# Two-tile blocks: where the split of the next block's second chunk, the copy out of PSUM and the row sums stand

## What is computed

```python
h = rmsnorm(x, pre_norm_mix)
z = h @ w_in                     # gated units, q, k, v, og, gates, m_a, m_b
y_a = spatial_gating(u, layernorm(vs), ...)
y_b = rmsnorm(gla_chunked(q, k, v, log_a)) * silu(og)
merged = sigmoid(m_a) * (y_a @ w_proj_a) + sigmoid(m_b) * (y_b @ w_proj_b)
x = x + rmsnorm(merged @ w_out, post_norm_mix)
q = rmsnorm(x, pre_norm_xa) @ wq;  k = rmsnorm(mem) @ wk;  v = rmsnorm(mem) @ wv
x = x + rmsnorm(softmax(q @ k.T) @ v @ wo, post_norm_xa)
hid = conv3(rmsnorm(x, pre_norm_ffn) @ w_up) + conv_b
gate, up = split(hid)
x = x + rmsnorm((gelu(gate) * up) @ w_down, post_norm_ffn)
```

## Time and profile before

| | us |
|---|---|
| median of 3 runs | 3876.51 (3867.89 to 3877.65) |
| the profiled execution, whole | 3870.68 |
| its span, first to last instruction | 3868.9 |
| TensorE busy within the span | 3625.0 |

### The profile page before, as it was taken

How to read it: one execution, slowest core, us unless ns; L and a number is a source line. 1 busy time by engine, 2 the same in 40 slices (tenths; PEclk the granted TensorE clock), 3 DMA queues, 4 the chain that set the end, 5 groups by cost and what they waited for, 6 DMA issues and landing times.

```text
span 3868.9 us, 46318 instructions
## 1 busy us (share of the span) xinstructions
PE 3625.0 (94%) x18672; PEld 2939.7 (76%) x18672; DVE 2013.4 (52%) x3121; ACT 1672.2 (43%) x2723; POOL 67.9 (2%) x118
## 2 busy tenths in 40 slices
PE   7899999999898999999999999999999799999998
PEld 2667777887776777777777777766777599999776
DVE  1666654344466746642355544445555466666444
ACT  2323344444422424455544334445445555555433
POOL 1200000000020000000000000000000000000000
PEclk8999999999999999999999999999999999999999
DMA  9643321233364455323355555534555256555554
GB/s 361 187 151 109 104 60 50 61 101 105 99 194 158 148 183 166 88 64 109 92 183 161 160 176 177 180 109 161 184 174 179 93 171 187 187 186 186 180 185 163
DMA packets 351045, 577.49 MB, mean 149 GB/s; under 512 B 25316, under 2 KB 131060, under 8 KB 348912
## 3 DMA queue, kind: packets, MB, share of 16 engines
q1 hardware_dynamic: 344512, 549.47, 44.8%
q0 software_dynamic: 6320, 25.06, 2.3%
HBM read 570.26 MB, written 4.19 MB: 148 GB/s over the span
## 4 chain that ended last, share of the span: by engine, by line
PE 56%; DVE 4%; ACT 3%; DMA 2%; issue 1%; DVEq 0%; SPq 0%; ACTq 0%
PE ps L706 36%; PE ps L1601 13%; PE ps L1283 1%; DVE w_lo L675 1%; DMA raw_ring<-in_w_in_dram 1%; ACT w_hi L669 1%; PE ps L1195 1%; PE ps L1081 1%; PE ps L1168 1%; PE ps L1177 0%; PE ps L743 0%; PE ps L1474 0%; PE ps L1479 0%; DMA raw_ring<-in_w_proj_b_dram 0%; PE ps L1191 0%
## 5 line engine op out<-in xcount | busy, mean ns | idle before, releaser
L675 DVE TENSOR_TENSOR w_lo<-raw_ring,w_hi 128x1024 fp32r<-128x1024 f32 (+1 forms) x827 | 1007.4, 1223 | 1173.5 <-ACT w_hi L669 1172.2
L669 ACT CAST w_hi<-raw_ring 128x1024 fp32r<-128x1024 f32 (+1 forms) x827 | 861.4, 1048 | 1218.2 <-PE ps L706 496.1
L706 PE MATMUL ps<-w_hi,r_a 128*128 128x512 f32 x3552 | 1311.6, 408 | 56.6 <-DVE w_lo L675 20.3
L706 PE MATMUL ps<-w_lo,r_a 128*128 128x512 f32 (+1 forms) x2624 | 1041.6, 397 | 0.0
L706 PE MATMUL ps<-w_hi,r_b 128*128 128x512 f32 (+1 forms) x2272 | 864.6, 399 | 17.6 <-DVE w_lo L675 10.8
L706 PEld LDWEIGHTS ps<-w_hi,r_a 128*128 128x128 f32 x3552 | 677.6, 191 | 242.6 <-issue 56.5
L706 PEld LDWEIGHTS ps<-w_lo,r_a 128*128 128x128 f32 x2624 | 502.4, 191 | 113.4 <-issue 8.1
L706 PEld LDWEIGHTS ps<-w_hi,r_b 128*128 128x128 f32 x2272 | 436.7, 192 | 126.6 <-DVE w_lo L675 16.5
L1601 PE MATMUL ps<-r_a,w_hi 128*128 128x256 f32 x2816 | 498.6, 279 | 0.0
L1601 PEld LDWEIGHTS ps<-r_a,w_hi 128*128 128x128 f32 x2816 | 430.8, 188 | 0.0
L1601 PE MATMUL ps<-r_a,w_lo 128*128 128x256 f32 x1408 | 394.5, 280 | 0.0
(11 more groups left out here) (335 smaller groups left out, 2949.9 us busy)
## 6 DMA issues: line engine op xcount, KB each, us to landing
raw_ring<-in_w_in_dram SPq DMA_DIRECT2D x386, 512.0 KB, 3.6
raw_ring<-in_ffn_w_up_dram SPq DMA_DIRECT2D x176, 512.0 KB, 3.5
raw_ring<-in_w_ada_dram SPq DMA_DIRECT2D x128, 512.0 KB, 3.8
raw_ring<-in_w_out_dram SPq DMA_DIRECT2D x96, 512.0 KB, 3.5
raw_ring<-in_ffn_w_down_dram SPq DMA_DIRECT2D x88, 512.0 KB, 3.5
gla_arena<-in_w_ada_dram SPq DMA_DIRECT2D x64, 512.0 KB, 9.2
raw_ring<-in_w_proj_b_dram SPq DMA_DIRECT2D x32, 512.0 KB, 3.5
raw_ring<-in_w_proj_a_dram SPq DMA_DIRECT2D x16, 512.0 KB, 3.5
```

Of the source, the lines that this page charges most:

```text
L669: nc.scalar.copy(WH[:, ph.s_slot(i, j), 0:n], RAW[:, ph.raw_slot(i, j), 0:n]).then_inc(hi_ready, 1)
L675: nc.vector.tensor_tensor(WL[:, ph.raw_slot(i, j), 0:n], RAW[:, ph.raw_slot(i, j), 0:n], WH[:, ph.s_slot(i, j), 0:n].bitcast(F32), ALU.sub ...
L706: mm = nc.tensor.matmul(PS[:, t, a:z], X(x, k, t), W[w][:, kk * cols + a:kk * cols + z], start=(k == 0 and q == 0), stop=(c == len(js) - 1 ...
```

## The change

It leaves every instruction of TensorE and its order; it changes where some instructions of ScalarE and VectorE stand, and two waits of TensorE. In the two-tile products the copy out of a block is put behind the split of the next block's second chunk. In "xk" the two sums of squares are put behind the third and the fourth split, and what hangs on them moves one chunk on, so that the last of four wide VectorE operations falls into "xv". In "down" the sums of squares go behind the fourth split. The pieces of the last "up" block are dealt between the first splits of "down"; TensorE waits for the block before the last alone, and for the last just ahead of chunk 21, which reads it.

```diff
@@ -1608,13 +1608,17 @@
             for i in range(11):
                 up_body(i)
 
-            pe.wait_ge(up_free, 88)
-            pe.wait_ge(up_lo, 44)
+            pe.wait_ge(up_free, 84)
+            pe.wait_ge(up_lo, 42)
 
             def dn_body(i):
                 for b in range(2):
-                    pe_block(pe, PH["down"], i, list(range(22 * b, 22 * b + 22)), 2, NB,
-                             lambda x, k, t: AT[:, x, k, t * P:t * P + P], range(2), acc_at("down", i, 2, b))
+                    js = list(range(22 * b, 22 * b + 22))
+                    for c in range(22):
+                        if (i, b, c) == (0, 0, 21):
+                            pe.wait_ge(up_lo, 44)
+                        pe_block_part(pe, PH["down"], i, js, c, 2, NB,
+                                      lambda x, k, t: AT[:, x, k, t * P:t * P + P], range(2), acc_at("down", i, 2, b))
             for i in range(2):
@@ -1680,7 +1684,7 @@
                 def body(i):
                     for q, j in enumerate(js):
                         act_hi(act, ph, i, j)
-                        if q == 0 and evac and i:
+                        if q == 1 and evac and i:
                             evac(i - 1)
                 for i in range(first, ph.iters):
@@ -2047,17 +2051,16 @@
                 ph = PH[name]
 
                 def body(i):
-                    if not (skip and i == 0):
-                        for j in range(9):
-                            act_hi(act, ph, i, j)
-                        sig_evac(name, i)
-                    for j in range(9, js):
+                    for j in range(9 if skip and i == 0 else 0, js):
                         act_hi(act, ph, i, j)
+                        if j == 9 and not (skip and i == 0):
+                            sig_evac(name, i)
                 for i in range(4):
                     body(i)
             act_hi(act, PH["ma"], 0, 0)
+            act_hi(act, PH["ma"], 0, 1)
             uv_evac(3)
-            for j in range(1, 4):
+            for j in range(2, 4):
@@ -2092,7 +2095,7 @@
             def q_body(i, evac, steps=()):
                 for j in range(8):
                     act_hi(act, ph, i, j)
-                    if j == 0 and evac:
+                    if j == 1 and evac:
@@ -2178,7 +2181,7 @@
             for i in range(4):
                 for j in range(0 if i else 9, 16):
                     act_hi(act, ph, i, j)
-                    if j == 8:
+                    if i and j == 9:
@@ -2192,7 +2195,7 @@
             for i in range(4):
                 for c in range(8):
                     act_hi(act, PH["wo2"], i, c)
-                    if i and c == 0:
+                    if i and c == 1:
@@ -2204,18 +2207,26 @@
             def x_evac(name, dst):
                 evac_to(name, PH[name], 7, 2, lambda t, b: dst[:, t, :])(0)
 
+            def y_squares(t):
+                ins = nc.scalar.activation(JUNK2, Y2[:, t], ACT.Square, accum_out=SS[:, t:t + 1])
+                if t == 0:
+                    L(ins)
+                else:
+                    ins.then_inc(ss_ready, 1)
+
             for j in range(8):
                 act_hi(act, PH["xk"], 0, j)
-                if j == 0:
+                if j == 1:
                     wo2_evac(3)
                     act.wait_ge(acc_free, AC["xk"][0][0])
                     act.wait_ge(rt_ready, NI["p_mix"])
-                    squares([(JUNK2, Y2[:, t], SS[:, t:t + 1]) for t in range(2)], ss_ready)
-                if j == 3:
+                if j in (2, 3):
+                    y_squares(j - 2)
+                if j == 4:
                     root("p_mix", SS[:, 0:2], RINV[:, 0:2])
             for j in range(8):
                 act_hi(act, PH["xv"], 0, j)
-                if j == 0:
+                if j == 1:
@@ -2241,24 +2252,28 @@
             warm_root()
             ph = PH["xo"]
 
-            def evac_squares(name, y, i, b, j):
+            def evac_y(name, y, i, b, j):
+                st, n = acc_at(name, i, 2, b), 2 * i + b
+                for t in range(2):
+                    gemm_wait(act, st, t, 2, PH[name], i, j)
+                    nc.scalar.copy(y[:, t, n * NB:n * NB + NB], PS[:, t, :]).then_inc(acc_free, 1)
+
+            def evac_squares(name, y, i, b):
                 st, n = acc_at(name, i, 2, b), 2 * i + b
                 cols = slice(n * NB, n * NB + NB)
-                for t in range(2):
-                    gemm_wait(act, st, t, 2, PH[name], i, j)
-                    nc.scalar.copy(y[:, t, cols], PS[:, t, :]).then_inc(acc_free, 1)
                 act.wait_ge(acc_free, st[0] + 2)
                 part_squares(y[:, 0, cols], 0, n, JUNKB)
                 part_squares(y[:, 1, cols], 1, n, JUNKB, y_sq if n < 3 else ss_ready)
 
             def xo_evac(i, b):
-                evac_squares("xo", Y2, i, b, 2 * b + 1)
+                evac_y("xo", Y2, i, b, 2 * b + 1)
+                evac_squares("xo", Y2, i, b)
             for i in range(2):
                 for b in range(2):
                     act_hi(act, ph, i, 2 * b)
+                    act_hi(act, ph, i, 2 * b + 1)
                     if i or b:
                         xo_evac(*((i, 0) if b else (i - 1, 1)))
-                    act_hi(act, ph, i, 2 * b + 1)
             act_hi(act, PH["up"], 0, 0)
             act_hi(act, PH["up"], 0, 1)
@@ -2315,22 +2330,26 @@
                             fn(pi, pb, q)
             for i in range(11):
                 up_body(i)
-            for c in range(8):
-                for fn, q in pieces.get(c, []):
-                    fn(10, 1, q)
-
-            ph = PH["down"]
+
+            pd = PH["down"]
 
             def dn_evac(i, b):
-                evac_squares("down", YF, i, b, 22 * b + 21)
+                evac_y("down", YF, i, b, 22 * b + 21)
             for i in range(2):
                 for b in range(2):
+                    before = (i, 0) if b else (i - 1, 1)
                     for q in range(22):
-                        act_hi(act, ph, i, 22 * b + q)
-                        if q == 0 and (i or b):
-                            dn_evac(*((i, 0) if b else (i - 1, 1)))
+                        act_hi(act, pd, i, 22 * b + q)
+                        if (i, b) == (0, 0):
+                            for fn, k in pieces.get(q, []):
+                                fn(10, 1, k)
+                        elif q == 1:
+                            dn_evac(*before)
+                        elif q == 3:
+                            evac_squares("down", YF, *before)
             warm_root()
             dn_evac(1, 1)
+            evac_squares("down", YF, 1, 1)
@@ -2390,7 +2409,7 @@
                     for q, j in enumerate(js):
                         if not (i == 0 and q < done):
                             dve_lo(dve, ph, i, j)
-                        for fn, at in ((evac, 1 if own else 0), (later, 3)):
+                        for fn, at in ((evac, 1), (later, 3)):
                             if fn and q == at and i:
@@ -3002,7 +3021,7 @@
             for i in range(4):
                 for j in range(0 if i else 9, 16):
                     dve_lo(dve, PH["mb"], i, j)
-                    if i and j == 0:
+                    if i and j == 1:
@@ -3038,21 +3057,20 @@
 
             for j in range(8):
                 dve_lo(dve, PH["xk"], 0, j)
-                if j == 2:
+                if j == 3:
                     mean_eps("p_mix", 2, D)
-                if j == 4:
+                if j == 5:
                     mean_rinv("p_mix", 2)
                     dve.wait_ge(pn_in, 16)
-                if j in (4, 6):
-                    t = (j - 4) // 2
-                    L(V.scalar_tensor_tensor(Y2[:, t], Y2[:, t], RINV[:, t:t + 1], PN, ALU.mult, ALU.mult))
                 if j in (5, 7):
                     t = (j - 5) // 2
-                    ins = TT(X2[:, t], X2[:, t], Y2[:, t], ALU.add)
-                    if t == 1:
-                        ins.then_inc(mixed, 1)
+                    L(V.scalar_tensor_tensor(Y2[:, t], Y2[:, t], RINV[:, t:t + 1], PN, ALU.mult, ALU.mult))
+                if j == 6:
+                    TT(X2[:, 0], X2[:, 0], Y2[:, 0], ALU.add)
             for j in range(8):
                 dve_lo(dve, PH["xv"], 0, j)
+                if j == 0:
```

More of the change, by code:

```diff
@@ L3040, in _ @@
                 dve_lo(dve, PH["xk"], 0, j)
-                if j == 2:
+                if j == 3:
                     mean_eps("p_mix", 2, D)
-                if j == 4:
+                if j == 5:
                     mean_rinv("p_mix", 2)
                     dve.wait_ge(pn_in, 16)
-                if j in (4, 6):
-                    t = (j - 4) // 2
-                    L(V.scalar_tensor_tensor(Y2[:, t], Y2[:, t], RINV[:, t:t + 1], PN, ALU.mult, ALU.mult))
                 if j in (5, 7):
                     t = (j - 5) // 2
-                    ins = TT(X2[:, t], X2[:, t], Y2[:, t], ALU.add)
-                    if t == 1:
-                        ins.then_inc(mixed, 1)
```

(5 more changed lines are left out.)

## The result

| | before | changed |
|---|---|---|
| median, us | 3877.08 (4 runs, 3867.89 to 3881.06) | 3846.39 (4 runs, 3840.55 to 3852.16) |
| ratio, 95% interval | | 0.9926 (0.9911 to 0.994) |
| span of the profiled execution | 3868.9 | 3849.4 |

The changed kernel is faster by 0.74%, some 29 us. The forecast was 3849.5. The spans differ by only 19.5 us, and the first question is why that is less.

What follows compares the result with a forecast made beforehand. TensorE, busy 3625.0 of 3868.9 us, bounds the kernel, so only its waits at edited places count. Eight terms sum to 27.0 us, taken from a median of 3876.5 to give 3849.5 us; range 3836 to 3862.

Steps and rivals of the forecast that it cites:

- Part 1: Plain block boundaries in "uv", "ma", "qkvo", "mb", "wo2": a stall of 0.35 us vanishes at 12.75 boundaries, +4.5 us.
- Part 2: Table loads going with the copy, first "uv" and third "mb" block: stall 0.65 instead of 0.35, twice, -0.6 us.
- Part 3: VectorE's copies in "ma" and "mb" come late: 2.0 and 2.6 us lost, -4.6; bounds nothing to a loss of 5.3.
- Part 4: "wo2": the turned tile goes ahead of the block's copy, removing TensorE's wait for transposed halves, +1.7 us.
- Part 5: "xk" and start of "xv": a 7.7 us loss shrinks to small losses of 0.7, +7.0 us; bounds 5 to 7.7.
- Parts 6 and 8: Block boundaries: "xo" three at 1.9 us, +5.7 (half, 2.9, if splits are late); "down" three at 1.84, +5.5.
- Part 7: From "up" to "down": 5.55 us wait for the first w_lo and 2.2 of half clock go, +7.8; lower end 6.5.
- (A): Rival: VectorE's six late copies bring the clock down, 2.8 us each; gain only 10, 3866 us; chance 0.05.
- (B): Rival: queues further behind than counted (table loads, late w_lo in "xv" or "xo"); gain 17 to 24; inside the forecast's 0.85.
- (C): Rival: the stall only moves, TensorE waits in the third chunk instead of the second; within 0.3%, 3870 us; chance 0.04.
- (D): Rival: late HBM transfers hold the second split and the copy behind it; 2.1 us to spare; slower, 3909; chance 0.03.

Runs made afterwards that it cites:

- One step too far: Changed kernel with copies behind the third split ("qkvo", "down"), "xk" squares together behind the second, last "up" pieces together behind the third; 3870.25 us, kernel before 3867.29.
- three slots: Three raw slots in "down" instead of five, put into the changed kernel (new order, 3873.3 us) and into the kernel before (old order, 3896.8 us).
- both times: The changed kernel profiled a second time, unaltered, beside the other kernels on one chip; ratio to the kernel before 0.9943.
- "xk" and "down" alone: Kernel before with only the changed orders of "xk" and of the block boundaries of "down"; ratio to the kernel before 0.9971.
- the best: Changed kernel with VectorE's "ma" and "mb" copies back behind the first split and both tables loaded early; 3840.63 us, ratio to the kernel before 0.9922.
- the rest alone: Changed kernel with "xk" and the block boundaries of "down" as they were before; ratio to the kernel before 0.9965.
- partial doses: Changed kernel with one "xk" square ahead of the second split, "mb" copies behind the third, "up" pieces two per split, four raw slots in "down"; 3859.51 us.

## Why the prediction was right

**The bound.** The reading that TensorE's waits at the edited places are the whole matter held: 27.3 us against 27.0, and every edited stage within 0.3. That the sums agree so closely is in part luck: 0.8 and -0.6 from slow matmuls, and -0.4 from a transfer in "mb", were not in the forecast and nearly cancel.

**Part 1** gave 4.5, as forecast: each "qkvo" boundary 0.35. **Part 2** gave -0.6: the gap is 0.79 us against the pace of 0.23, with 0.08 in the matmul behind it 0.64 in place of 0.35, twice; the row of the load shows the copy 0.01 us behind it. (So the trace has the load of the Trainium skill's page "ScalarE: Activation LUTs", "What ACT_TABLE_LOAD costs", at 1.28, and nothing of the drain that the page adds; an estimate from the page's 2.66 would make the stalls 1.9.) **Part 3** gave -4.4 instead of -4.6: in "ma" a boundary costs 0.51 and 0.08 behind it, and not 0.67. In "mb" it was 0.87 a boundary to the hundredth, because a row of the same order stood in the trace of before. That is the difference between a term that was read and one that was put together. (The lower bound of this part doesn't come out of its own terms: 3 x 1.24 in "ma" and 2.6 in "mb" are a loss of 6.3, not 5.3. And 4.6 + 0.7 + 2 + 4 above the forecast lead to 3838, not 3836. Neither bound was reached.)

**Part 4** was 1.7. **Part 5** was 7.3 instead of 7.0: VectorE's w_lo for the second chunk of "xv" was 0.20 us late and not 0.5; with the matmul behind it the small losses came to 0.3 instead of 0.7. The timeline of VectorE has it between the last two wide operations and after them:

```profile
2973.41 1.23 DVE L675 TENSOR_TENSOR w_lo<-raw_ring,w_hi 128x1024 fp32r<-128x1024 f32 x1
2974.55 2.29 DVE L3073 TENSOR_TENSOR f_arena<-f_arena 128x2048 f32<-128x2048 f32 x1
2976.75 2.35 DVE L675 TENSOR_TENSOR w_lo<-raw_ring,w_hi 128x1024 fp32r<-128x1024 f32 x2
```

The first of the last two w_lo ends near 2977.95 and TensorE was due at 2977.83. **Parts 6 and 8** came out at 5.7 and 5.6, as forecast to 0.1: no split in "xo" was late, so the half that its bound gave up was not lost. **Part 7** was 7.7, 5.56 of it the wait and the rest the slow matmuls.

**Not in the sum:** 0.8 us in the attention behind "xq" and -0.6 at the start of "up", both from the number of slow matmuls there. Neither belongs to a part of the change, see below.

**The rivals.** (A), the clock, fell for waits of 1.24 us; waits of 4.03 in the same places were followed by slow matmuls each time, at some 1.4 us and not 2.8. (B) did not show: the copy came 0.01 us behind the load, and w_lo in "xv" was less late than forecast. (C) was wrong for the kernel; the lumps of "One step too far" do what it says, for about a third of the stall or less and not for all of it. (D) was the right mechanism with too little behind it. Landings were 4.3 us in "down" and not 3.5, so of the 2.1 us to spare 1.3 was left; no boundary waited. With three slots the new order was 4.1 us slower in "down".

## What to carry to other kernels

When work must stand between the steps that feed an engine, there is a window for it: not ahead of a step whose time is short, and not behind a step that itself waits for the end of what the work is to release. Count for each step when it can first begin and when it is last needed, on each queue by itself: here the right place for ScalarE's copy was wrong for VectorE's, which hangs on a further step. A long piece needs to be dealt out, not only moved, or a part of the stall comes back one chunk later.

## What the runs showed that was not expected

Whether slow matmuls follow a wait of TensorE is not fixed by the wait's length. In the second block's products of all ten traces, none followed the 79 gaps of 1.4 to 2.05 us between two matmuls; they followed 18 of the 33 gaps of 2.16 to 2.84 us and all 19 of 4.26 to 5.68, 6 to 14 of them at 0.43 us. The same gap in the same kernel can do either: of six equal gaps of 2.17 in "qkvo" two were followed, of three in "down" none. And the wait of 4.68 us in the attention behind "xq", which the change leaves alone, was followed by 11 slow matmuls in the kernel before, 6 in the changed one (both times), 7 with "xk" and "down" alone, 12 in the best and 10 with the rest alone: that is the 0.8 us of the table. What sets the number the runs don't show.

A chunk's landing in "down" had a median of 3.5 or 3.6 us in some executions (before, the rest alone, the kernels one step too far, with partial doses and with three slots) and 4.3 in others (the changed kernel twice, the best, "xk" and "down" alone). It changes within an execution too: in the kernel before, the transfers issued in the second block of "down" have a median of 4.3 and those of the three others 3.4 to 3.5; in the changed kernel the first block has 3.6 and the others 4.3. What it hangs on the runs don't show. So five slots were enough at every landing time seen here, and four were not at one boundary.
